# Where the sums of six norms are formed, and in which order the first two weight chunks after a norm are worked through, in a two-block transformer kernel on one Trainium2 core

## The chip, the cores and the metric

The kernel runs on one core of one Trainium2 chip. The metric is the device time of one execution in microseconds (us). The core has TensorE (PE, with its weight loads shown as PEld), VectorE (DVE), ScalarE (ACT), GpSimd (POOL) and the DMA queues, of which SyncE (SP) issues most.

## The reference

Two transformer blocks run one after the other on 512 tokens of 1024 features in float32. The first has sparse and stick-breaking attention, a mixture of 32 experts and a gated per-layer input, and ends with an RMS norm. The second puts 16 meta tokens ahead (528 tokens) and has two layers:

```python
h = jnp.concatenate([meta, x], axis=1)
for l in range(DEPTH_2):
    ...
    h = _layernorm(DN_ALPHA * h + mix, ln_mix_g[l], ln_mix_b[l])
    f = jnp.square(jax.nn.relu(h @ mlp_w1[l])) @ mlp_w2[l]
    h = _layernorm(DN_ALPHA * h + f, ln_mlp_g[l], ln_mlp_b[l])
return h[:, N_META:]

def _layernorm(x, g, b):
    mu = jnp.mean(xf, axis=-1, keepdims=True)
    xc = xf - mu
    var = jnp.mean(jnp.square(xc), axis=-1, keepdims=True)
    return (xc * lax.rsqrt(var + EPS_2) * g + b).astype(x.dtype)

def _rmsnorm(x, g):
    y = xf * lax.rsqrt(jnp.mean(xf * xf, axis=-1, keepdims=True) + EPS)
    return (y * g.astype(jnp.float32)).astype(x.dtype)
```

The change concerns the four layer norms of the second block and two RMS norms of the first: the one ahead of the router (`ffn_norm`) and the final one.

## The kernel before, in words

**Layout.** Features lie on the 128 partitions, so an activation is 8 tiles of 128 features by 512 or 528 tokens: `X` (`residual`), `HN` (`normed`); `XA` and `HA` are their last 512 columns. A sum over the features goes over partitions and over 8 tiles. PE forms it with a matrix of ones (`ONES`) as weights: 8 matmuls of 512 columns, or 16 of 264 (two halves of 528), add up in one PSUM bank or two, and every partition has the sum. A float32 matmul stands as two records in the trace; one on rounded `fp32r` operands as one.

**Weights.** They come in chunks of 128 x 1024 (8 feature tiles by 128 outputs) through a ring `RING` of 8 slots. SP refills a slot when PE has begun the chunk after the one in it (`chunk_begun`).

**High and low parts.** In the last two thirds of the second block (both MLPs and the odd layer's projections) every product is three cheap `fp32r` matmuls: high weight by high activation, low weight by high activation, high weight by low activation. ACT makes a weight chunk's high half (`high`, L1553), POOL subtracts it for the low half (`low_parts`, L2237), PE waits for that in `take_parts` (L420). ACT and POOL convert a chunk while PE works on the one before: `high` waits until chunk n-1 has begun. The places (`IN_MLP`, `IN_ODD`) hold two chunks.

**A layer norm** (PE L760 or L770, ACT L1534, DVE L1620):
1. DVE adds each output tile to the residual (`accumulate`, L1611) as PE finishes it.
2. After the last chunk PE sums the 8 residual tiles (L766 for 512 columns, L780 for 528).
3. DVE scales the sum to the mean in SBUF (L1624, L1626), then subtracts it from each tile (L1628).
4. ACT squares each tile (L1540), PE sums the squares (`norm_sum`, L469), ACT forms the inverse deviation with Ln and Exp (L1188, L1189).
5. ACT converts the first chunk of the next stage (L1557); DVE scales the tiles (L1634); for each tile ACT adds the bias twice, for `X` (L1548) and rounded for `XH` or `XHO` (L1550), and DVE subtracts to get the low half (L1639).
6. PE takes the first chunk of the next stage tile by tile (`fresh`): for each of the 8 it waits for the low half, then does all three products.

The four are called here mix 0, MLP 0 (528 tokens), mix 1 and MLP 1 (512 tokens). MLP 1 ends the kernel, and has only steps 1 to 4, the scaling and one bias.

**The two RMS norms.** ACT squares each residual tile when DVE has added it (L1182, L1295); PE sums the 8 squares after the stage's last chunk, at L574 and L642 through `norm_sum`.

**MLP.** 16 chunks up, 16 down, twice. In the up part ACT evacuates with Relu (L1571, L1573), and DVE squares and splits (L1785 to L1787).

The order on each engine is the order of the code; semaphores alone tie them.

## Time and profile before

| | |
|---|---|
| runs, median of 3 | 2762.01 us (2761.5 to 2762.05) |
| the profiled execution | 2744.34 us, span 2742.6 us |
| PE busy | 2586.7 us, 94% of the span, 11768 matmuls |
| DVE, ACT, POOL busy | 788.4, 693.1 and 597.0 us (29%, 25%, 22%) |
| granted TensorE clock, mean | 0.96 of full speed |
| DMA | 275.33 MB, 100 GB/s on average |

PE is at 94%, but this is a mean over stages. A norm is a place at which PE has, for some 20 us each time, only sums and waits, and there the rows of the timeline tell what is waited for. All rows quoted further down are from the profiled execution.

### The profile page before, as it was taken

The numbers are of one execution on the slowest core, as the hardware profiler recorded it, in microseconds if no ns is written. First come the engines' busy times: TensorE is split into PE (matmuls) and PEld (weight loads), VectorE is DVE, ScalarE is ACT, GpSimd is POOL, SyncE is SP. The second block draws the span as 40 slices with busy tenths as digits, with TensorE's granted clock in tenths as the row PEclk, the third lists the DMA queues.
The fourth block names the chain that finished last, engine by engine and source line by source line (L and its number), as shares of the span: only waits on it lengthen the run. The fifth ranks groups of instructions, "written<-read, shape, count | busy, mean of one in ns | idle before, by whom it ended". The sixth has DMA issues, their size and how long they took to land.

```text
span 2742.6 us, 30358 instructions
## 1 busy us (share of the span) xinstructions
PE 2586.7 (94%) x11768; PEld 1758.7 (64%) x11768; DVE 788.4 (29%) x1294; ACT 693.1 (25%) x1116; POOL 597.0 (22%) x362
## 2 busy tenths in 40 slices
PE   7999999899799979998989999989999999899998
PEld 3446554445433334785679999978877567677875
DVE  0551332111311122234136216135100231640622
ACT  1302224410111121145232222132322231421222
POOL 0000001110011100011004344324433013344442
PEclk9799998899799989999999999999999999999999
DMA  3121110034589952220012222222222012222220
GB/s 139 47 77 65 42 49 10 0 118 174 221 324 356 387 238 70 73 77 8 31 39 93 85 91 86 84 70 93 93 84 77 24 43 81 71 91 92 92 92 31
DMA packets 68261, 275.33 MB, mean 100 GB/s; under 512 B 12440, under 2 KB 12568, under 8 KB 55872
## 3 DMA queue, kind: packets, MB, share of 16 engines
q1 hardware_dynamic: 59648, 260.01, 25.7%
q0 software_dynamic: 8512, 13.89, 1.5%
q8 instruction: 74, 1.21, 0.2%
q14 instruction: 27, 0.22, 0.0%
HBM read 321.02 MB, written 16.80 MB: 123 GB/s over the span
## 4 chain that ended last, share of the span: by engine, by line
PE 45%; issue 22%; POOL 6%; DVE 1%; ACT 1%; DMA 1%; POOLq 0%; SPq 0%; DVEq 0%
PE ps L739 14%; PE ps L754 13%; PE ps L1121 6%; POOL weights_low L2243 5%; PE ps L723 3%; PE ps L1143 3%; PE ps L637 2%; PE ps L469 1%; PE ps L1107 1%; PE ps L661 1%; PE ps L629 1%; DMA area<-pair_rows 0%; POOL parts L2243 0%; PE ps L1129 0%; PE ps L780 0%
## 5 line engine op out<-in xcount | busy, mean ns | idle before, releaser
L754 PE MATMUL ps<-parts 128*128 128x512 f32 x1920 | 486.1, 398 | 26.1 <-DVE parts L1639 13.6
L2243 POOL TENSOR_TENSOR parts<-weights,parts 128x1024 fp32r<-128x1024 f32 x128 | 325.5, 2543 | 632.2 <-ACT parts L1557 632.2
L739 PE MATMUL ps<-parts 128*128 128x264 f32 x3328 | 425.9, 286 | 16.2 <-DVE parts L1787 6.8
L754 PEld LDWEIGHTS ps<-parts 128*128 128x128 f32 x1920 | 364.7, 190 | 118.2 <-issue 24.5
L739 PEld LDWEIGHTS ps<-parts 128*128 128x128 f32 x3328 | 417.7, 191 | 17.7 <-issue 15.6
L1557 ACT ACTIVATE parts<-weights 128x1024 fp32r<-128x1024 f32 x192 | 202.8, 1056 | 427.3 <-PE ps L739 155.5
L2243 POOL TENSOR_TENSOR weights_low<-weights,parts 128x1024 fp32r<-128x1024 f32 x64 | 156.5, 2445 | 317.8 <-ACT parts L1557 317.8
L1121 PE MATMUL ps<-area,normed 128*64 128x512 f32 x752 | 172.8, 601 | 1.6 <-DVE normed L1975 1.6
L1787 DVE TENSOR_TENSOR parts<-normed,parts 128x528 f32 (+1 forms) x64 | 159.0, 2484 | 9.4 <-DVE normed L1786 2.1
L458 PE MATMUL ps<-normed,weights 128*128 128x512 f32 x288 | 125.7, 599 | 3.1 <-DVE normed L1609 2.4
L1121 PEld LDWEIGHTS ps<-area,normed 128*64 128x64 f32 x752 | 56.3, 139 | 112.5 <-issue 110.3
L1022 PE MATMUL ps<-normed,weights 128*128 128x512 f32 x256 | 121.0, 616 | 0.0
L1617 DVE SCALAR_TENSOR_TENSOR residual<-residual,ps 128x528 f32<-128x528 f32 (+3 forms) x32 | 22.3, 696 | 295.0 <-PE ps L739 90.2
L458 PEld LDWEIGHTS ps<-normed,weights 128*128 128x128 f32 x288 | 55.2, 192 | 73.5 <-issue 70.8
L919 PE MATMUL ps<-parts 128*128 128x512 f32 (+1 forms) x320 | 99.8, 393 | 0.8 <-ACT area L1378 0.8
L723 PE MATMUL ps<-residual,weights 128*128 128x264 f32 x416 | 93.4, 386 | 2.6 <-DVE residual L1609 2.4
L1193 ACT ACTIVATE area<-ps 128x512 f32<-128x512 f32 (+2 forms) x71 | 42.1, 599 | 195.0 <-PE ps L458 117.2
L723 PEld LDWEIGHTS ps<-residual,weights 128*128 128x128 f32 x416 | 78.9, 190 | 17.1 <-issue 3.8
L1143 PE MATMUL ps<-area 128*64 128x512 f32 x376 | 87.7, 599 | 1.3 <-DVE area L1983 1.3
L1615 DVE TENSOR_TENSOR residual<-residual,ps 128x512 f32<-128x512 f32 (+2 forms) x32 | 21.5, 691 | 230.1 <-PE ps L739 91.2
L1022 PEld LDWEIGHTS ps<-normed,weights 128*128 128x128 f32 x256 | 47.1, 194 | 62.3 <-issue 61.8
L2120 POOL TENSOR_SCALAR_AFFINE_SELECT area<-area 128x128 f32<-128x128 f32 x68 | 20.2, 304 | 298.2 <-DVE area L1859 243.2
(371 smaller groups left out, 3180.7 us busy)
## 6 DMA issues: line engine op xcount, KB each, us to landing
weights<-in_weights SPq DMA_DIRECT2D x283, 512.0 KB, 3.5
area<-in_experts SPq DMA_DIRECT2D x141, 1024.0 KB
area<-pair_rows SPq DMA_DIRECT2D x4, 1024.0 KB, 8.0
residual<-in_x SPq DMA_DIRECT2D x1, 2048.0 KB, 9.7
area<-bias_scratch POOLq DMA_DIRECT2D x1, 2048.0 KB, 8.6
token_rows<-area SPq DMA_DIRECT2D x1, 2048.0 KB, 6.6
out_tiles<-residual SPq DMA_DIRECT2D x4, 512.0 KB, 2.8
area<-in_decay POOLq DMA_DIRECT2D x2, 528.0 KB, 3.8
```

Source lines behind the costliest of these rows:

```text
L458: ins = mm(ps[:, b], wt[:, k], rhs(k), start=k == 0, stop=k == DT - 1)
L637: ins = mm(ps[:, 4 + n], wt[:, k], HA[:, k], start=k == 0, stop=k == DT - 1)
L723: ins = mm(ps[:, b + h, 0:HALF], wt[:, k], rhs(m * DT + k)[:, HALF * h:HALF * h + HALF], start=m == k == 0, stop=m == len(chunks) - 1 and ...
L739: ins = mm(ps[:, b + h, 0:HALF], wt[:, k], x[:, m * DT + k, HALF * h:HALF * h + HALF], start=m == k == j == 0, stop=m == chunks - 1 and k ...
L754: ins = mm(ps[:, b], wt[:, k], x[:, m * DT + k, META:T2], start=m == k == j == 0, stop=m == chunks - 1 and k == DT - 1 and j == 2)
L919: ins = mm(ps[0:kw, banks[j]], x[:, 2 * m + k, c:c + kw], wt[:, 512 * k:512 * k + 512], start=m == k == n == 0, stop=m == 3 and k == 1 and ...
L1022: ins = mm(ps[:, 5 + (u // 2) % 2], gate.wt[:, k], HA[:, k], start=k == 0, stop=k == DT - 1)
L1121: ins = mm(ps[WIN * side:WIN * side + WIN, n % 2], XW[n % 2][:, 4 * j + k, WIN * side:WIN * side + WIN], wt, start=j == k == 0, stop=j == ...
L1143: ins = mm(ps[WIN * side:WIN * side + WIN, 4 + h], HIDT[n % 2][:, f, WIN * side:WIN * side + WIN], wt, start=f == 0, stop=f == 1)
L1557: fn(place[0][n % 2], RING[:, n % SLOTS], ACT.Copy).then_inc(S["w_hi"], 1)
L1787: v.tensor_tensor(FL[:, at, first:T2], f, FH[:, at, first:T2], ALU.subtract).then_inc(S["dve_evac"], 1)
L2243: g.tensor_tensor(low, RING[:, n % SLOTS], place[0][n % 2], ALU.subtract).then_inc(S["w_lo"], 1)
```

## The change

1. **Feature sums by DVE.** The new `total` lets DVE add up tiles 0 to 6 in `R` while PE is still in the stage; PE sums `R` and tile 7 alone. The matrix is `MEAN` (1/1024 instead of 1), and DVE subtracts straight from PSUM, without the step that scaled the mean.
2. **Two RMS sums in two groups.** The same for the squares: `rms_sum`.
3. **Four chunks converted ahead.** `IN_MLP` holds four high halves, low halves go to `RING_LOW`. Before a layer norm ACT and POOL convert the next stage's first four chunks, without waiting on `chunk_begun`. In the up part ACT evacuates tile j, then converts chunk j + 4.
4. **First two chunks together.** `first_pair`: PE waits for the high half of each activation tile and does both high products for both chunks; then the low activation products of both. ACT makes the eight high halves first, the eight `X` tiles after; DVE scales all eight tiles, then makes the eight low halves from `HN` and the bias in one step each.

The core of the diff:

```diff
@@ the places
-        FH, FL = part(0, 16, N2), part(8448, 16, N2)
-        XH, XL = part(16896, DT, N2), part(21120, DT, N2)
-        IN_MLP = [[part(25344 + D * j, D) for j in range(2)], [part(25344 + D * (2 + j), D) for j in range(2)]]
+        XH, XL = part(0, DT, N2), part(4224, DT, N2)
+        FH, FL = part(12544, 16, N2), part(20992, 16, N2)
+        IN_MLP = [[part(8448 + D * j, D) for j in range(4)], None]
+        EARLY = {use_of("odqk") + 2 + j: part(D * j, D) for j in range(2)}
@@ PE
-                norm_sum(8, SEQ, 7, lambda t: HN[:, t])
+                rms_sum(HA[:, DT - 1])
...
-                norm_sum(8, SEQ, 7, lambda t: MERGED[:, t], at=0)
+                rms_sum(MERGED[:, DT - 1])
...
+            def first_pair(high, low, place, cols):
+                banks = [2 * bank() for _ in range(2)]
+                pair = [take_parts(place) for _ in range(2)]
+                for k in range(DT):
+                    pe.wait_ge(S["x_hi"], w.next("x_hi"))
+                    for c in range(2):
+                        for h, at, width in cols:
+                            for j in range(2):
+                                ins = mm(ps[:, banks[c] + h, 0:width], pair[c][j][:, k], high[:, k, at:at + width],
+                                         start=k == j == 0, stop=False)
...
+                for c, k in [(c, k) for k in range(DT - 2) for c in range(2)] + [(c, k) for c in range(2) for k in (DT - 2, DT - 1)]:
+                    if c == 0:
+                        pe.wait_ge(S["x_lo"], w.next("x_lo"))
+                    for h, at, width in cols:
+                        ins = mm(ps[:, banks[c] + h, 0:width], pair[c][0][:, k], low[:, k, at:at + width],
+                                 start=False, stop=k == DT - 1)
...
+            def layer_norm(cols):
+                pe.wait_ge(S["sum_part"], w.next("sum_part"))
+                for j, src in enumerate((R, X[:, DT - 1])):
+                    if j:
                         pe.wait_ge(S["dve_evac"], w.value("dve_evac"))
-                    ins = mm(ps[:, 0], ONES, XA[:, t], start=t == 0, stop=t == DT - 1)
+                    for h, at, width in cols:
+                        x = R[:, at - cols[0][1]:at - cols[0][1] + width] if j == 0 else src[:, at:at + width]
+                        ins = mm(ps[:, h, 0:width], MEAN, x, start=j == 0, stop=j == 1)
                 ins.then_inc(S["norm_sum"], 1)
...
+            def rms_sum(last):
+                pe.wait_ge(S["sum_part"], w.next("sum_part"))
+                mm(ps[:, 7], ONES, R[:, 0:SEQ], start=True, stop=False)
+                pe.wait_ge(S["norm_sq"], w.next("norm_sq", 8))
+                mm(ps[:, 7], ONES, last, start=False, stop=True).then_inc(S["norm_sum"], 1)
@@ ACT
+                act.wait_ge(S["lru_done"], 4)
+                for j in range(4):
+                    high(use_of("up0") + j, slots=-1)
                 layer_norm("mix", 0)
...
+                act.wait_ge(S["y_lo"], 16)
+                for j in range(4):
+                    high(use_of("up1") + j, slots=-1)
                 layer_norm("mix", 1)
...
-                if kind == "mix":
-                    high(use_of(f"up{l}"))
-                elif l == 0:
-                    high(use_of("odqk"), place=IN_ODD)
+                parts = XH if kind == "mix" else XHO if l == 0 else None
+                if parts is not None:
+                    for t in range(DT):
+                        act.wait_ge(S["norm_out"], w.next("norm_out"))
+                        fn(parts[:, t, T2 - T:], h[:, t], ACT.Identity, bias=vec(f"ln_{kind}_b", 8 * l + t)).then_inc(S["x_hi"], 1)
...
@@ ACT, mlp
-                            high(n + j, i)
                             if w.counted("dve_evac", 7):
...
                             w.count("dve_evac")
+                            high(n + j, i)
...
-                for j in range(7):
+                for j in range(4):
                     high(n - 8 + j)
+                if l == 0:
+                    for j in range(4):
+                        high(use_of("odqk") + j, place=IN_ODD, slots=-1)
                 layer_norm("mlp", l)
@@ DVE
+            def total(n, x, T, name, waits):
+                if 1 <= n < DT - 1:
+                    dve.wait_ge(S[name], waits)
+                    ins = v.tensor_tensor(R[:, 0:T], x[:, 0] if n == 1 else R[:, 0:T], x[:, n], ALU.add)
...
             def layer_norm(kind, l):
-                    step(v.tensor_scalar(two(R[:, :]), halves(0), 1.0 / D, None, ALU.mult))
                 for t in range(DT):
-                    v.tensor_tensor(h[:, t], x[:, t], R[:, 0:T], ALU.subtract).then_inc(S["ln_cent"], 1)
+                        ins = v.tensor_tensor(two(h[:, t]), two(x[:, t]), halves(0), ALU.subtract)
...
-                        v.tensor_tensor(low, x[:, t - 2], high, ALU.subtract).then_inc(S["x_lo"], 1)
+                        v.scalar_tensor_tensor(out=low, in0=h[:, t], scalar=vec(f"ln_{kind}_b", 8 * l + t), in1=high,
+                                               op0=ALU.add, op1=ALU.subtract).then_inc(S["x_lo"], 1)
...
+                v.tensor_scalar(MEAN, NONES, -1.0 / D, None, ALU.mult)
...
                     accumulate(XA[:, n], ps[:, n % 4], 1.0)
+                    total(n, HA, SEQ, "norm_sq", 8 + 1 + n + 1)
...
                     accumulate(XA[:, n], HT[n % 2], 1.0)
+                    total(n - 1, MERGED, SEQ, "norm_sq", 8 + 1 + 8 + 8 + n)
...
                     accumulate(two(X[:, n]), halves(2 * (n % 4)), ALPHA)
+                    total(n, X, T2, "dve_evac", w.next("dve_evac"))
```

The order of the instructions changes at three places that the prediction speaks of.

PE at mix 0, before (`area` is the stage's last operand, `residual` is `X`, `parts` the high and low halves):

```order
L723 MATMUL ps<-area,weights 128x264 x128
L780 MATMUL ps<-residual,matrices 128x264 x16
L469 MATMUL ps<-residual,matrices 128x264 x16
L739 MATMUL ps<-parts 128x264 x768
L135 UNCONDITIONAL_BRANCH
```

and with the change (`rstd` is `R`; the pair of rows at L771 comes 32 times in all):

```order
L729 MATMUL ps<-area,weights 128x264 x128
L796 MATMUL ps<-rstd,matrices 128x264 x2
L796 MATMUL ps<-residual,matrices 128x264 x2
L474 MATMUL ps<-residual,matrices 128x264 x16
L771 MATMUL ps<-parts 128x264
L771 MATMUL ps<-parts,weights_low 128x264
...
L779 MATMUL ps<-parts 128x264 x32
L743 MATMUL ps<-parts 128x264
L743 MATMUL ps<-parts,weights_low 128x264
```

The first sum falls from 16 matmuls to 4. The first two chunks are 64 products with high activations and then 32 with low ones.

DVE at mix 0, before:

```order
L1617 SCALAR_TENSOR_TENSOR residual<-residual,ps 128x528 x8
L1626 TENSOR_SCALAR rstd<-ps 128x528
L1628 TENSOR_TENSOR normed<-residual,rstd 128x528 x8
L1634 SCALAR_TENSOR_TENSOR normed<-normed,vectors,rstd 128x528 x3
L1639 TENSOR_TENSOR parts<-residual,parts 128x528
L1634 SCALAR_TENSOR_TENSOR normed<-normed,vectors,rstd 128x528
L1639 TENSOR_TENSOR parts<-residual,parts 128x528
```

and with the change:

```order
L1654 SCALAR_TENSOR_TENSOR residual<-residual,ps 128x528
L1661 TENSOR_TENSOR rstd<-rstd,residual 128x528
L1654 SCALAR_TENSOR_TENSOR residual<-residual,ps 128x528
L1674 TENSOR_TENSOR normed<-residual,ps 128x528 x8
L1679 SCALAR_TENSOR_TENSOR normed<-normed,vectors,rstd 128x528 x8
L1688 SCALAR_TENSOR_TENSOR parts<-normed,vectors,parts 128x528 x8
```

Six additions stand between the accumulations, the scaled mean is gone, and the low halves come after all scalings.

ACT at MLP 0, before:

```order
L1557 ACTIVATE parts<-weights 128x1024 x7
L1535 ACT_TABLE_LOAD
L1540 ACTIVATE residual<-normed 128x528 x8
L1188 ACTIVATE rstd<-ps,vectors 128x528
L1189 ACTIVATE rstd<-rstd 128x528
L1557 ACTIVATE parts<-weights 128x1024
L1548 ACTIVATE residual<-normed,vectors 128x528
```

and with the change:

```order
L1593 ACTIVATE parts<-weights 128x1024 x8
L1570 ACT_TABLE_LOAD
L1575 ACTIVATE residual<-normed 128x528 x8
L1215 ACTIVATE rstd<-ps,vectors 128x528
L1216 ACTIVATE rstd<-rstd 128x528
L1581 ACTIVATE parts<-normed,vectors 128x528 x8
L1585 ACTIVATE residual<-normed,vectors 128x528 x8
```

The conversion that stood between the inverse deviation and the biases now stands ahead of the norm.

## Rows read from the trace of the kernel before

**Rows 1.** The page, busy time of each engine.
```profile
PE 2586.7 (94%) x11768; PEld 1758.7 (64%) x11768; DVE 788.4 (29%) x1294; ACT 693.1 (25%) x1116; POOL 597.0 (22%) x362
```
**Rows 2.** Timeline, mix 0: start us, length us, engine, line, operation [idle before, releaser].
```profile
1402.93 7.28 PE L780 MATMUL ps<-residual,matrices 128*128 128x264 f32 x32
1403.13 0.70 DVE L1617 SCALAR_TENSOR_TENSOR residual<-residual,ps 128x528 f32<-128x528 f32 x1 [6.42 <-PE ps L723]
...
1410.99 5.04 DVE L1628 TENSOR_TENSOR normed<-residual,rstd 128x528 f32<-128x528 f32 x8
...
1412.43 9.08 PE L469 MATMUL ps<-residual,matrices 128*128 128x264 f32 x32 [2.22 <-ACT residual L1540]
...
1422.28 0.64 ACT L1189 ACTIVATE rstd<-rstd 128x528 f32<-128x528 f32 x1
1422.83 1.04 ACT L1557 ACTIVATE parts<-weights 128x1024 fp32r<-128x1024 f32 x1
1422.95 4.22 DVE L1634 SCALAR_TENSOR_TENSOR normed<-normed,vectors,rstd 128x528 f32<-128x528 f32 x3 [6.92 <-ACT rstd L1189]
...
1427.94 8.93 PE L739 MATMUL ps<-parts 128*128 128x264 f32 x48 [6.43 <-DVE parts L1639]
...
1438.50 11.76 PE L739 MATMUL ps<-parts 128*128 128x264 f32 x95 [1.63 <-POOL parts L2243]
```
**Rows 3.** Timeline, MLP 0.
```profile
1825.00 5.04 DVE L1628 TENSOR_TENSOR normed<-residual,rstd 128x528 f32<-128x528 f32 x8
...
1834.60 0.64 ACT L1189 ACTIVATE rstd<-rstd 128x528 f32<-128x528 f32 x1
...
1850.82 0.50 PE L754 MATMUL ps<-parts 128*128 128x512 f32 x1 [1.67 <-POOL weights_low L2243]
```
**Rows 4.** Timeline, mix 1, and the chain of waits: up chunks 2 to 16.
```profile
2337.07 0.63 ACT L1189 ACTIVATE rstd<-rstd 128x512 f32<-128x512 f32 x1
...
2342.65 8.70 PE L754 MATMUL ps<-parts 128*128 128x512 f32 x24 [6.34 <-DVE parts L1639]
...
2353.04 83.68 PE ps L754 x360
```
**Rows 5.** Timeline, MLP 1, the end of the kernel.
```profile
2715.38 7.03 PE L766 MATMUL ps<-residual,matrices 128*128 128x512 f32 x16
...
2723.17 4.90 DVE L1628 TENSOR_TENSOR normed<-residual,rstd 128x512 f32<-128x512 f32 x8
...
2733.13 5.39 DVE L1634 SCALAR_TENSOR_TENSOR normed<-normed,vectors,rstd 128x512 f32<-128x512 f32 x8 [5.06 <-ACT rstd L1189]
2733.92 5.36 ACT L1548 ACTIVATE residual<-normed,vectors 128x512 f32<-128x512 f32 x8 [0.82 <-DVE normed L1634]
```
**Rows 6.** Timeline, the sums of squares ahead of the router and of the final norm.
```profile
661.46 0.63 ACT L1182 ACTIVATE normed<-residual 128x512 f32<-128x512 f32 x1 [6.24 <-DVE residual L1615]
661.52 7.10 PE L469 MATMUL ps<-normed,matrices 128*128 128x512 f32 x16 [0.83 <-issue]
...
1104.00 7.11 PE L469 MATMUL ps<-area,matrices 128*128 128x512 f32 x16 [2.25 <-issue]
```
**Rows 7.** PE by stretches: us, PE busy (records), granted clock, DMA share, GB/s.
```profile
1412.40:1421.50 9.10, 9.07 (x32) 0.81 0.00 0
...
1427.90:1437.00 9.10, 8.91 (x48) 0.69 0.17 58
...
1826.40:1833.80 7.40, 7.36 (x32) 1.00 0.35 135
...
1529.20:1535.00 5.80, 5.80 (x35) 0.72 0.27 92
```
**Rows 8.** Timeline, one tile of the up part of the first MLP.
```profile
1521.64 2.72 POOL L2243 TENSOR_TENSOR parts<-weights,parts 128x1024 fp32r<-128x1024 f32 x1 [3.07 <-ACT parts L1557]
1522.25 2.67 DVE L1787 TENSOR_TENSOR parts<-normed,parts 128x528 f32 x1
1525.81 0.61 ACT L1573 ACTIVATE normed<-ps 128x528 f32<-128x528 f32 x1 [4.24 <-PE ps L739]
```

159 lines of the change are left out of this document (83 added, 76 removed).

## The prediction

> **What bounds the kernel now.** The page comes first: PE is busy 94% of the span [rows 1], so what is not PE's work gains nothing unless PE waits for it. The waits sorted by releaser and the chain of waits then lead to the norms. There the timeline shows, at mix 0 [rows 2]: when its last chunk is done, PE sums 8 residual tiles for 7.28 us. After that it waits for the centring and the first square, sums the squares, waits 6.43 us for the first low half, and does the first chunk in 8.93 us, although 48 such matmuls take 5.88 us when nothing holds them (95 take 11.76 in the last row: 0.1225 us each is used below, 0.12 to 0.125 with its ends). It then waits another 1.63 us for POOL, which converts the second chunk late. The same pattern is at MLP 0 and mix 1 [rows 3, 4], and its first half at the end of the kernel [rows 5]. Two RMS norms have the long sum alone [rows 6]. All this is on the path: PE is the engine that ends last, and it waits or sums there.
>
> **1. The residual sum and the scaled mean.** Before, from the end of the last chunk (1402.93) to the start of the centring (1410.99) mix 0 needs 8.06 us. With the change PE has the sum of tiles 0 to 6 before the last chunk ends, if DVE's six additions stay hidden: each is a tile operation like those of 0.70 us, in gaps of 6.42 us between accumulations [rows 2]. PE sums `R` in 4 records, 4 x 7.28 / 32 = 0.91 us, beside DVE's last accumulation, which ends at 1403.83. With 0.1 us for the semaphore and 0.91 us for tile 7, the centring starts at 1404.95: 6.0 us sooner. MLP 0 has the same 528 columns: 6.0. With 512 columns [rows 5] it is 2723.17 - 2715.38 = 7.79 us before, and 0.2 + 0.70 + 0.1 + 2 x 7.03 / 16 = 1.9 us after: 5.9 each at mix 1 and MLP 1. **Sum 23.8 us.** The centring from PSUM takes 0.70 us a tile (the accumulation that reads PSUM) instead of 0.63 [rows 2]. PE's sum of squares takes 0.91 us a tile and stays the slower one, so this costs the first tile's 0.07 us, counted as nothing.
>
> **2. The first two chunks.** Count from the end of Exp, s.
> - Before: mix 0 has s = 1422.92, and its second chunk ends at 1438.50 + 5.88 = 1444.38, s + 21.5. MLP 0: s = 1835.24; the second chunk starts at 1850.82, and 24 matmuls of 0.232 us (83.68 / 360, [rows 4]) end at 1856.4, s + 21.2. Mix 1: s = 2337.70, end 2353.04 + 5.6 = 2358.6, s + 20.9.
> - After: the first scaling is done at s + 0.8 and ACT's first high half at s + 1.55 (the last norm's two rows start 0.03 and 0.82 after its Exp, at 0.67 a tile [rows 5]). PE starts at s + 1.65. Then 96 matmuls follow without a gap: 11.8 us for 528 columns, and 48 of 0.232, 11.1 us, for 512. The ends are s + 13.4 and s + 12.8.
> - Why no gap: in the high phase PE needs 8 x 0.1225 = 0.98 us a tile and gets one every 0.7. The low halves begin at s + 5.6 (8 scalings) and are all there at s + 11.3. PE comes to tile 7 of the first chunk at about s + 12. The four conversions are done ahead, so no POOL operation of 2.72 us [rows 8] stretches the scalings, as one does now, where three take 4.22 us instead of 2.1 [rows 2].
>
> Gains 8.1, 8.4 and 8.1: **24.6 us.** Chunk 5 is due at s + 25; its conversion starts after the first evacuation (s + 14) and needs 1.04 + 2.72 us. It is late by nothing. The late `X` biases (eight of ACT's, until about s + 12.5) end before that evacuation.
>
> **3. The two RMS sums.** 16 records take 7.10 us [rows 6]. After: the router's `R` sum runs 661.52 to 662.4, while the last square ends at 662.09; the end is 663.3 instead of 668.6, gain 5.3. At the final norm the sixth addition stands on DVE behind the last accumulation, with which PE's start at 1104.00 is tied, and adds 0.7 before PE may start; two matmuls then end at 1106.5 instead of 1111.1, gain 4.6. **9.9 us.** The router and the experts follow in sequence, with PE's own waits, so I let this pass through whole.
>
> **4. The clock.** PE's idle time costs more than itself. The granted clock is 0.81 during the square sum of mix 0, which takes 9.08 us for 7.3 of work, and 0.69 in the first chunk after; after the 3.4 us stop between up and down part it is 0.72 for 5.8 us, 1.6 us lost [rows 7]. These are mixtures of 2.4 and 1.2 GHz. Now low clock in the first chunk is covered, as PE waits for low halves anyway. With the change PE starts sooner, is dense, and pays: bounds are 0 (at MLP 0 the square sum, behind a 2.2 us wait too, ran at 1.00 [rows 7]) and 3.4 us, twice the 1.6. I take 1.3 at each of three pairs, nearest the 1.6 row, 1.2 at the even layer's start, where 7.1 us of PE work ahead becomes 1.8, 0.2 at the router and 0.8 over the four square sums. **Cost 6.1 us.**
> The Trainium skill (TensorE: Matmul & The Clock Gate, "HAM oscillation — how this bites in real kernels") says that waits between bursts of matmuls throttle the engine again at each burst. It speaks against this change, which shortens the bursts between unchanged waits, and is the first rival.
>
> **5. At nothing:** the 12 early conversions (ACT and POOL work that moves, hidden behind stages of eight or more chunks); the swap of evacuation and conversion in the up part, since the trace shows that order in effect already, `chunk_begun` holding the conversion back; POOL's three DMA issues at MLP 0, behind four more conversions at most. `total` at mix 1 is the exception: five conversions run back to back there, 5 x 2.72 us, over the last two chunks. DVE's two-SBUF operation beside POOL takes 2.67 instead of 0.7 us [rows 8], so the sixth addition can be late by up to 3 us: kept for the range. The centring reads one operand from PSUM, as the accumulations do that show 0.70 us.
>
> **Sum:** 23.8 + 24.6 + 9.9 - 6.1 = 52.2 us. The profiled execution, 2744.3 us, becomes 2692. The median of the runs lies 17.7 us above it, 0.6%; I take the same distance, so 2762.0 - 52.2 = **2709.8 us**.
>
> **Rivals.**
> - *The clock takes the gain back (15%).* Every square sum and every pair runs at 1.2 GHz: 4 x 3.5 us (half of 7.3 us' work done at half speed), 3 x 3.4, and 1.7 each at router and even layer, 28 us instead of my 6. Time 2762 - 58 + 28 = 2732. For it: mix 0 shows 0.81 even after a long sum. Against: behind the same wait it was 1.00 at MLP 0 [rows 7], and at MLP 1 the 9.96 us from the first centring to the scalings leave room for a sum at full speed alone [rows 5].
> - *The clock costs nothing (10%).* The 58.3 us come whole, and mix 0's square sum gets its 1.7 us back: 2702.
> - *Conversion and split collide for good: slower (3%).* In the up part DVE's split of a tile ends with POOL's conversion, at 1524.92, and the next evacuation is done at 1526.4 [rows 8]; 1.5 us is free. If the new order or the ring's shorter lead of four chunks pushes ACT, POOL or DVE over PE's 5.8 us a chunk by x, each of 64 up chunks pays x. It outweighs 52 us from x = 0.8. At x = 1.0 the time is 2762 + 12 = 2774. Against: POOL needs 2.7 of the 5.8 us.
> - *The gain is absorbed (2%).* Were the sums' time covered by another wait, as a router or expert stage that waits for DMA, parts 1 to 3 would give little: 2760.
> - *The forecast (70%)*, 2702 to 2722.
>
> The Trainium skill (SBUF — State Buffer, "SBUF: two separate sides") says that a GpSimd operation and a VectorE one with two SBUF inputs exclude each other for a whole instruction; rows 8 agree. By it alone mix 1 would be 2 to 3 us later, 2712.
>
> **How the numbers follow.** Point 2710. The bounds of the clock term (0 to 28) and mix 1's 3 us give 2702 to 2735; leaving out the tail of the first rival and all below 2700, the range is 2700 to 2726, for 80%. A change within 0.2% (5.5 us) is about what this kernel's measurement can't tell from none. Faster by more: forecast, both clock rivals and half a percent of others, 0.95; same 0.02; slower 0.03.
>
> **What would show it.** In the new profile: 4 records (528) or 2 (512) of `MEAN` ahead of each centring, started within 2 us after the last chunk; no scaled mean; first-pair matmuls from 1.7 us after Exp and both chunks done 13 us after it; no wait on POOL there; 4 records instead of 16 at the RMS sums; the granted clock of the square sums and pairs says what part 4 costs. Wrong would be: a PE wait for `R`; waits on high halves between tiles; a new wait on POOL in the up part; or a clock at 0.5 through a whole pair.

## The result

| | before | after |
|---|---|---|
| runs, median | 2762.03 us (2761.5 to 2767.18, 4 runs) | 2693.43 us (2691.6 to 2693.95, 4 runs) |
| the profiled execution | 2744.34 us, span 2742.6 us | 2693.95 us, span 2692.2 us |
| granted TensorE clock, mean | 0.96 | 0.96 |

The change makes the kernel faster, ratio 0.9746 (95% interval 0.9729 to 0.9763), by 68.6 us. 2710 us was forecast, 2700 to 2726 as the range: the time lies 6.6 us below it. Yet between the two profiled executions there are only 50.4 us, against a forecast sum of 52.2. The rest of this text is about these two figures.

The page of the changed kernel, first part (before: [rows 1]):

```profile
PE 2555.0 (95%) x11672; PEld 1740.8 (65%) x11672; DVE 811.0 (30%) x1327; ACT 692.9 (26%) x1116; POOL 596.5 (22%) x362
```

PE has 96 records less and is busy for 31.7 us less; the rest of the 50.4 us was waiting. Timeline of the changed kernel at mix 0 (before: [rows 2]; start us, length us, engine, line, operation [idle before, releaser]):

```profile
1401.90 1.05 PE L796 MATMUL ps<-rstd,matrices 128*128 128x264 f32 x4
1402.11 0.70 DVE L1654 SCALAR_TENSOR_TENSOR residual<-residual,ps 128x528 f32<-128x528 f32 x1 [5.61 <-PE ps L729]
1402.86 1.16 PE L796 MATMUL ps<-residual,matrices 128*128 128x264 f32 x4
1404.06 5.01 DVE L1674 TENSOR_TENSOR normed<-residual,ps 128x528 f32<-128x528 f32 x8 [1.25 <-PE ps L796]
...
1405.49 7.39 PE L474 MATMUL ps<-residual,matrices 128*128 128x264 f32 x32 [1.47 <-ACT residual L1575]
...
1413.65 0.64 ACT L1216 ACTIVATE rstd<-rstd 128x528 f32<-128x528 f32 x1
1414.33 5.52 DVE L1679 SCALAR_TENSOR_TENSOR normed<-normed,vectors,rstd 128x528 f32<-128x528 f32 x8 [5.26 <-ACT rstd L1216]
1415.13 5.49 ACT L1581 ACTIVATE parts<-normed,vectors 128x528 fp32r<-128x528 f32 x8 [0.84 <-DVE normed L1679]
1416.01 0.56 PE L771 MATMUL ps<-parts 128*128 128x264 f32 x1 [3.13 <-ACT parts L1581]
```

From the start of PE's sum to the centring it is 2.16 us in place of 8.06. The three scalings that took 4.22 us beside POOL are now part of eight that take 5.52, and PE opens the pair 1.7 us after the end of Exp. The squares keep the shape they had. The centring from PSUM takes 5.01 us for eight tiles, 0.63 each as before, where 0.70 had been taken.

Mix 1, at the point where `total` was thought to come late (before: [rows 4]):

```profile
2286.52 2.87 DVE L1661 TENSOR_TENSOR rstd<-rstd,residual 128x512 f32<-128x512 f32 x1
...
2290.97 1.02 PE L796 MATMUL ps<-rstd,matrices 128*128 128x512 f32 x2
2291.17 0.69 DVE L1654 SCALAR_TENSOR_TENSOR residual<-residual,ps 128x512 f32<-128x512 f32 x1 [1.78 <-PE ps L991]
```

The sixth addition is stretched to 2.87 us beside POOL, as [rows 8] had led one to fear, but PE is still in the last chunk, and the stretch costs nothing.

The two RMS sums of the changed kernel (before: [rows 6]; the rows of L1215 are ACT's Ln, which waits for the sum; the router's is L1188 at 668.66 in the kernel before):

```profile
667.75 0.63 ACT L1209 ACTIVATE normed<-residual 128x512 f32<-128x512 f32 x1 [6.17 <-DVE residual L1652]
669.81 0.69 ACT L1215 ACTIVATE rstd<-ps,vectors 128x512 f32<-128x512 f32 x1 [1.43 <-PE ps L808]
...
1104.53 1.33 PE L806 MATMUL ps<-rstd,matrices 128*128 128x512 f32 x2 [2.93 <-DVE rstd L1661]
1105.65 1.91 PE L808 MATMUL ps<-area,matrices 128*128 128x512 f32 x2
1107.61 0.69 ACT L1215 ACTIVATE rstd<-ps,vectors 128x512 f32<-128x512 f32 x1 [2.91 <-PE ps L808]
```

PE by stretches in the changed kernel, with the granted clock behind POOL's column (before: [rows 7]; columns: us, then the busy time of PE, PEld, DVE, ACT and POOL with their counts, granted clock, DMA share, GB/s). They are mix 0's squares, the opening of its pair, and the openings of the pairs of MLP 0 and mix 1:

```profile
1405.40:1412.90 7.50, 7.39 (x32) 6.00 (x32) 3.67 (x6) 4.34 (x8) 0.00 (x0) 1.00 0.01 2
1416.00:1419.30 3.30, 3.29 (x15) 3.30 (x16) 3.30 (x6) 3.30 (x6) 0.00 (x0) 0.50 0.40 148
...
1814.70:1818.00 3.30, 3.23 (x9) 2.54 (x10) 3.30 (x6) 3.30 (x6) 0.00 (x0) 0.58 0.43 145
...
2304.70:2308.00 3.30, 3.30 (x14) 2.69 (x15) 3.30 (x6) 3.30 (x6) 0.00 (x0) 1.00 0.46 154
```

Two pairs open at about half clock, one does not, and the square sum of mix 0, at 0.81 before, is at 1.00. One place that the prediction priced at 1.2 us stands out: the even layer's projections, right behind the final norm. Their first 10 us in the kernel before, in the changed kernel, and in a second trace of the changed kernel (a0 below), each from its own first matmul:

```profile
1113.49:1123.49 10.00, 10.00 (x45) 8.57 (x46) 9.66 (x18) 0.61 (x1) 5.15 (x6) 1.00 0.49 149
1109.95:1119.95 10.00, 9.99 (x33) 8.11 (x34) 9.66 (x18) 0.00 (x0) 5.15 (x6) 0.72 0.41 134
1108.65:1118.65 10.00, 10.00 (x32) 8.13 (x33) 9.66 (x18) 0.00 (x0) 5.15 (x6) 0.72 0.40 134
```

### The profile page after: what moved, and what is told of

Its sections match the earlier page's. It is cut to its first block, busy times and chain, and to the rows that moved or that the text cites. A ratio compares the mean times of both kernels' runs of the same rounds, so it can differ in the third digit from the quotient of the medians.

```text
span 2692.2 us, 30120 instructions
## 1 busy us (share of the span) xinstructions
PE 2555.0 (95%) x11672; PEld 1740.8 (65%) x11672; DVE 811.0 (30%) x1327; ACT 692.9 (26%) x1116; POOL 596.5 (22%) x362
## 3 DMA queue, kind: packets, MB, share of 16 engines
q1 hardware_dynamic: 59648, 260.01, 26.1%
## 4 chain that ended last, share of the span: by engine, by line
PE 66%; issue 3%; DVE 2%; POOL 2%; ACT 1%; DMA 1%; SPq 0%; DVEq 0%; POOLq 0%; ACTq 0%
PE ps L756 15%; PE ps L743 13%; PE ps L1148 6%; PE ps L729 6%; PE ps L946 4%; PE ps L991 3%; PE ps L1170 3%; PE ps L642 2%; PE ps L973 2%; POOL weights_low L2301 2%; PE ps L474 1%; PE ps L893 1%; PE ps L909 1%; PE ps L771 1%; PE ps L962 1%
## 5 line engine op out<-in xcount | busy, mean ns | idle before, releaser
L2301 POOL TENSOR_TENSOR weights_low<-weights,parts 128x1024 fp32r<-128x1024 f32 x192 | 481.8, 2512 | 898.3 <-ACT parts L1593 898.3
L756 PE MATMUL ps<-parts 128*128 128x512 f32 x1344 | 422.3, 394 | 9.0 <-DVE parts L1842 6.7
L743 PE MATMUL ps<-parts 128*128 128x264 f32 x2240 | 409.9, 285 | 8.1 <-DVE parts L1842 6.9
L743 PEld LDWEIGHTS ps<-parts 128*128 128x128 f32 x2240 | 348.4, 189 | 8.7 <-issue 8.7
L743 PE MATMUL ps<-parts,weights_low 128*128 128x264 f32 x1120 | 318.6, 284 | 0.0
L756 PEld LDWEIGHTS ps<-parts 128*128 128x128 f32 x1344 | 253.3, 188 | 70.1 <-issue 10.4
L756 PE MATMUL ps<-parts,weights_low 128*128 128x512 f32 x672 | 266.2, 396 | 0.0
L743 PEld LDWEIGHTS ps<-parts,weights_low 128*128 128x128 f32 x1120 | 212.5, 190 | 0.0
L756 PEld LDWEIGHTS ps<-parts,weights_low 128*128 128x128 f32 x672 | 126.4, 188 | 29.4
L1654 DVE SCALAR_TENSOR_TENSOR residual<-residual,ps 128x528 f32<-128x528 f32 (+1 forms) x32 | 22.3, 696 | 282.2 <-PE ps L743 90.1
L463 PEld LDWEIGHTS ps<-normed,weights 128*128 128x128 f32 x288 | 54.6, 190 | 72.6 <-issue 70.1
```

What stands on the lines that cost most here:

```text
L463: ins = mm(ps[:, b], wt[:, k], rhs(k), start=k == 0, stop=k == DT - 1)
L743: ins = mm(ps[:, b + h, 0:HALF], wt[:, k], x[:, m * DT + k, HALF * h:HALF * h + HALF], start=m == k == j == 0, stop=m == chunks - 1 and k ...
L756: ins = mm(ps[:, b], wt[:, k], x[:, m * DT + k, META:T2], start=m == k == j == 0, stop=m == chunks - 1 and k == DT - 1 and j == 2)
L2301: g.tensor_tensor(RING_LOW[:, n % SLOTS], RING[:, n % SLOTS], high_slot(n, place), ALU.subtract).then_inc(S["w_lo"], 1)
```

## The experiments

**Both kernels again.** The distance between the profiled execution and the median, which the forecast had carried over, was tried first.

> The kernel before, unchanged, to learn why its timed executions lie at 2762 us and its profiled one at 2744 us, a distance I had carried over to the changed kernel, which does not have it. Theory 1 (execution by execution the TensorE clock falls at other places, above all in the attention stages from 243 to 547 us, where PE waits a little in each unit): the executions spread between 2744 and 2767 us, and the slower ones have a mean granted clock 0.01 lower; the profile's stages differ in length where the granted clock differs. Theory 2 (something outside the clock that only this kernel has, in one stage): all executions near 2762 us at the clock 0.96, and one stage is about 18 us longer than in the earlier profile at the same granted clock. Theory 3 (the first profile was shortened by chance of the launch, not by a stage): stages of equal length, span and time apart by more than 2 us.

Measured: 2755.22 us (2749.77 to 2769.45, 12 runs) against 2753.41 (2744.42 to 2766.84, 17 runs) of the same kernel: ratio 1.001 (0.999 to 1.0031). The kernel before has no one time. Over the comparisons of this study it was timed 103 times more: 12 executions lie at 2744.0 to 2745.6 us with mean granted clock 0.960, 44 at 2749.6 to 2756.0 with 0.956 or 0.957, 11 at 2757.0 to 2759.4 with 0.954 or 0.955, and 36 at 2761.5 to 2773.1 with 0.947 to 0.951. The profiled one of the forecast was of the first kind, the runs beside it of the last. The five comparisons ran on five chips, and in each the executions of one kernel spread over at least 19 us, so that the spread is not one between chips. This is theory 1.

The trace taken here is of the second kind (2751.79 us). At the router's sum it is 3.4 us behind the first profile, at the first score 4.7, and 7.5 when the scores and what follows them at once are done; that is its whole distance. The last step, before and here (the matmuls right behind the scores):

```profile
1267.85 2.77 PE L827 MATMUL ps<-matrices,area 128*97 128x128 f32 x24 [0.95 <-DVE area L2086]
1273.60 4.51 PE L827 MATMUL ps<-matrices,area 128*97 128x128 f32 x24 [0.95 <-DVE area L2086]
```

> The changed kernel, unchanged, for more executions. The kernel before gave 2744 to 2769 us in 29 executions, its time falling with the mean granted clock (0.960 at 2744, 0.948 at 2769). Theory 1 (chance of the draws: both kernels have the same attention stages, in which the clock varies): the changed kernel spreads likewise, from about 2690 to 2712, median near 2700, and the gain is about 52 us as worked out from the two profiles. Theory 2 (the change also ends the spread): all executions lie within 3 us of 2693, and the gain is 60 us against the median of before.

Measured: 2693.22 us (2687.37 to 2695.99, 6 runs), before 2761.93 (17 runs), ratio 0.9757 (0.9723 to 0.9792). The changed kernel's ten executions lie within 9 us, those of the kernel before within 29. That is nearer to theory 2 (all within 3 us of 2693) than to theory 1 (2690 to 2712). So the gain is 57 us from fastest to fastest, 50 from profile to profile, and near 69 between these medians.

**The parts alone.** Sums only (feature sums and RMS sums, the rest as before); early conversion and the pair only; early conversion only.

```diff
@@ a1, from the kernel before
-                norm_sum(8, SEQ, 7, lambda t: HN[:, t])
+                rms_sum(HA[:, DT - 1])
...
-                layer_norm()
+                layer_norm(HALVES)
@@ a2, from the changed kernel
-                rms_sum(HA[:, DT - 1])
+                norm_sum(8, SEQ, 7, lambda t: HN[:, t])
...
+                for t in range(DT):
...
+                        ins = mm(ps[:, h, 0:width], ONES, X[:, t, at:at + width], start=t == 0, stop=t == DT - 1)
@@ a3, from a2
-                first_pair(XHO, XLO, IN_ODD, TOKENS)
-                for n in range(6):
-                    linear_parts(1, XHO, XLO, IN_ODD)
+                for n in range(8):
+                    linear_parts(1, XHO, XLO, IN_ODD, fresh=n == 0)
```

> Parts 1 and 2 alone (feature sums and squares added up by VectorE, mean in the matrix); chunks, conversion and first chunk as before. My working: 23.8 us from the four layer norms and 8 to 10 from the two RMS sums, so 30 to 33 us less than before, and in the profile the centring starts about 2.1 us after the last chunk's end instead of 8.06. Rival (the gain of the sums is mostly given back, since less TensorE work ahead lets the clock fall in the square sums and first chunks): 20 us or less, with granted clocks of 0.5 to 0.8 in the four square sums.

> Parts 3 and 4 alone (four chunks ahead, high products of two chunks first), sums as before. My working: second chunk done 13 to 15 us after Exp instead of 21, at three norms: 20 to 25 us less than before. If the parts add up, this and the sums alone give 52 together. Rival (the two parts interact: with a long sum ahead the clock holds through the pair): 25 us here, and more than the whole change has left over.

> Part 3 alone: four chunks converted ahead, but the first chunk tile by tile as before, with all three products, ScalarE and VectorE in the old order, old sums. Removed are the first conversion behind Exp (1 us of ScalarE, 2.7 us of GpSimd that held up three scalings by 2.1 us) and the wait for the second chunk (1.6 us): 3 x (2.1 + 1 + 1.6), some 12 to 14 us less than before, if the clock doesn't change. Rival (the second chunk's wait was covered by something else that now shows, the first chunk at 1.3 us a tile): 8 us or less.

Measured: a1 2719.28 us (2713.66 to 2720.2, 6 runs), ratio 0.9849 (0.9815 to 0.9884); a2 2735.51 (2723.75 to 2745.26, 6), 0.9905 (0.9868 to 0.9942); a3 2743.57 (2740.28 to 2756.88, 12), 0.9954 (0.9928 to 0.9979). The fastest execution of each, against 2744.4 for the fastest kind of the kernel before, has clean parts: 30.7, 20.6 and 4.1 us. The first two are as expected, and agree with what the traces show of the places themselves (below). a3 is a miss: 12 to 14 us were expected and its rival had 8 or less. Its trace has the second chunk of mix 0 done 18.5 us after Exp (1463.0) in place of 21.5, 3.0 us gained where 4.7 were worked out: the wait for the second chunk is gone, but the first still takes until 12.7 us after Exp, 1.2 us less than before. Three such norms would give 9 us; where the other 5 went is not shown. The pair makes 16 us more out of the early conversion.

The traces of the two slowest, a2 and a3, share a stretch that no other trace had until then. Groups of PE instructions between 1210 and 1330 us, the score matmuls of the even layer's attention (`pe_mla`, 40 tasks): before, then a2, then the changed kernel (busy us, mean ns | idle before, releasers):

```profile
L816 PE MATMUL ps<-area 96*16 96x16 f32 (+5 forms) x96 | 25.1, 382 | 6.9 <-DVE area L2086 5.5 <-ACT area L1305 0.8
```

```profile
L834 PE MATMUL ps<-area 96*16 96x16 f32 (+5 forms) x96 | 40.6, 588 | 6.4 <-DVE area L2127 5.6 <-ACT area L1323 0.8
```

```profile
L843 PE MATMUL ps<-area 96*16 96x16 f32 (+5 forms) x96 | 24.9, 381 | 6.9 <-DVE area L2143 5.5 <-ACT area L1332 0.8
```

The same 96 records take 15.5 us more. PE by stretches, 1240 to 1270 us, before and in a2:

```profile
1240.00:1270.00 30.00, 23.83 (x101) 13.76 (x101) 20.94 (x82) 16.05 (x25) 6.41 (x7) 1.00 0.00 1
```

```profile
1240.00:1270.00 30.00, 26.10 (x62) 14.59 (x61) 13.52 (x55) 13.74 (x22) 7.65 (x8) 0.50 0.00 1
```

The clock is 1.00 (2.4 GHz) in the one and 0.50 (1.2 GHz) in the other. Nothing of the change acts here. PE sits idle 0.8 us ahead of the scores, for ACT's last evacuation, and up to 0.8 us in each of the eight heads, for DVE.

**Does the RMS part, or the start of the scores, decide it?** The RMS part alone, the layer norm part alone (both as in the diffs above), and matmuls ahead of the scores that put them off:

```diff
@@ c3 (n = 5), c4 (n = 10, kernel before), d1 (n = 2)
                 pe.wait_ge(S["k_ready"], 1)
+                for _ in range(n):
+                    mm(ps[:, 4, 0:HALF], IDENT, X[:, 0, 0:HALF], start=True, stop=True)
                 for u in range(5 * HEADS):
```

> The kernel before with the two RMS sums in two groups alone. Seven traces so far show what parts the executions of a kernel: in the two at the lowest mean clock (2743.5 and 2754.0 us of span) the forty score tasks of the even stage's attention ran at granted clock 0.50 from 2.5 us after their first matmul on, and the score matmuls took 46.2 us; in the five others they took 31.1 to 32.3 us. Theory A (the start of the scores decides): the RMS sums move the start of the scores by some us, and no execution falls into the slow kind: 2744.4 (the fast kind of the kernel before) less 8.5 = 2736 median, all of its executions within 2731 to 2745, though the median of the kernel before lies 5 to 18 us above its fast kind. Theory B (the parts only add up, the spread is chance): as many slow ones as before, 8.5 us under the median of the kernel before, executions spread over 20 us or more.

> The changed kernel with the two RMS sums as they were; the scores of the even stage's attention start then where they do in the kernel before. Theory A (the start of the scores decides): both kinds occur, 2744.4 less 46 = 2698 where the scores keep their clock and some 15 us more, 2713 to 2718, where they lose it; spread of the executions over 12 us, median more than 8.5 us above the changed kernel's. Theory B (the parts only add up): 2693.4 and 8.5 = 2702 us, within 5 us like the changed kernel.

> The changed kernel with five matmuls of 128x264 more, into a bank that nobody reads, right ahead of the first score matmul of the even stage's attention: 1.2 us of work (0.24 us each, from the 32 such matmuls that take 7.66 us ahead of them). Theory A (the start of the scores decides): they push the start of the scores to where the two slow traces had it; the scores take 46 us in place of 31, and the time is 2693.4 and 1.2 and 15 = 2710 us in all or most executions. Theory B: 2694.6 us, scores 31 us. If neither, the clock does not depend on the start to a microsecond.

> The kernel before with ten such matmuls more at the same place: 2.4 us of work. Theory A (the start of the scores decides): the scores of most executions start past the bad spot (which spans a microsecond or two) and the time falls in spite of the work: median 2747 to 2752, under that of the kernel before, scores 31 us in the trace. Theory B: slower by 2.4 us, the same spread as the kernel before. A third outcome, all slow (2764 and more), would say that the bad spot is wider than 2.4 us.

Measured: c1 2747.28 us (2737.72 to 2752.3, 12 runs); c2 2711.67 (2702.13 to 2719.34, 6); c3 2691.45 (2687.38 to 2702.4, 6); c4 2756.54 (2751.43 to 2771.64, 12), beside 2752.16 for the kernel before. c2 came as theory A had it, with three executions at 2702 to 2706 us and three at 2717 to 2719. The others did not. c1 should by theory A have been free of the stretch, and its trace has it in full (96 records, 40.7 us; 2750.94 us); its fastest executions, 2737.7, are 6.7 us under the fastest of the kernel before. c3 did not lose the clock: its trace, of its slowest execution, has the scores at 24.9 us. c4 was slower, by 4.4 us where its ten matmuls take 4.7. Its trace, of a fast execution, has the scores at full clock, but four others lie at 2768 to 2772 with a mean clock of 0.949 or 0.950, 16 to 20 us above its fastest, about what the stretch costs; none of them was traced. So the RMS sums do not cure it, the start alone does not bring it on in the changed kernel, and in the kernel before 4.7 us of dense matmuls between the wait and the scores do not keep it away in every execution. c3 also taught that five such matmuls are 2.49 us, not 1.2: each is two records.

> The changed kernel with two matmuls of 128x264 more ahead of the first score matmul. The trace of the run with five showed that such a matmul is two instructions and takes 0.49 us, so that five were 2.5 us and not 1.2; two are 1.0 us. Theory A (the start of the scores decides, in a spot about a microsecond wide that the five stepped over): the scores take 46 us in place of 31 and the time is 2693.4 and 1 and 15 = 2709 us in most executions. Theory B (the start has nothing to do with it): 2694.4 us, scores 31 us.

Measured: 2694.39 us (2690.63 to 2704.12, 6 runs), scores 24.9 us. Theory A in its first form falls. But the added matmuls, which stand behind the wait of 0.79 us, had also kept PE busy until the scores began. So the idle time itself was put to the test.

**The idle time filled.** One matmul goes into PE's wait ahead of the scores, one into the wait of each head:

```diff
+                pe.wait_ge(S["act_evac"], w.value("act_evac", 1))
+                mm(ps[:, 6, 0:HALF], IDENT, X[:, 0, 0:HALF], start=True, stop=True)
                 pe.wait_ge(S["act_evac"], w.value("act_evac"))
...
+                    if t == 1:
+                        mm(ps[:, 4, 0:HALF], IDENT, X[:, 0, 0:HALF], start=True, stop=True)
                     if u >= 2:
                         pe.wait_ge(S["smax"], w.next("smax"))
```

> The kernel of c1_rms_only, whose scores lost their clock in ten executions of twelve by its times (2743 to 2752 against 2737.7), with one matmul of 128x264 in the 0.79 us in which TensorE waits for ScalarE ahead of the scores, and one in each head ahead of its second score matmul, where TensorE waits 0.8 us for VectorE: nine matmuls of 0.49 us, all but the first head's in idle time. Theory A (TensorE loses its clock there because it does too little as the scores begin): the clock holds, scores 31 to 32 us, median 2738 to 2739 and the executions within 5 us or so of it, 8 or 9 us under c1_rms_only. Theory B (the fall has another cause than the engine's idle time): 2748 us and the same spread as c1_rms_only, and with it TensorE's fillers at half clock on the path, some us more.

> The kernel before with the same nine matmuls. Theory A: its executions at mean clock 0.951 and below (2761 to 2773 us) vanish, the rest stay at 2744 to 2754; median 2745 to 2752. Theory B: 2753 to 2762, spread as before. Should theory A hold here and in d2, the 17.7 us by which the median of the kernel before lay above its profiled execution were this one stretch.

Measured, d3: 2750.29 us, ratio 0.9976 (0.9956 to 0.9996). One execution at 13381 us stands apart and is left out; the other eleven lie at 2744.3 to 2752.0. In the same comparison 10 of 23 executions of the kernel before were at 2757 us and above; at 2761 us and above, where the expectation drew the line, there were five, and by these alone eleven executions would tell little. The traces of d2 and d3 have the scores at full clock (24.8 us). d2: 2743.25 us (2737.67 to 2748.72, 12 runs), 4 us under c1 where 8 or 9 were expected; no execution is in c1's upper range of 2750 to 2752, but seven lie between 2743 and 2749, four of them further off than the 5 us that were allowed. The one profiled there, 2744.19 us, is slow elsewhere (0.956 on the mean). The fillers are a cure for the one stretch and not for the spread as a whole. Which of the nine does it, the first or those in the heads, these two runs do not part.

**The idle time made longer, in the kernel that never lost its clock.** ACT does one (e1) or two (e2) more sigmoids ahead of the evacuation that PE waits for; e3 is e2 with four matmuls in the wait.

```diff
@@ e1 (k = 1), e2 and e3 (k = 2), ACT
-                    evac2([(ALL, out[:, n % 4])], ACT.Sigmoid, bias=vec(bias, n % 4))
+                    evac2([(ALL, JUNK[j]) for j in range(k) if n == 7] + [(ALL, out[:, n % 4])], ACT.Sigmoid, bias=vec(bias, n % 4))
@@ e3, PE
+                pe.wait_ge(S["act_evac"], w.value("act_evac", 1))
+                for _ in range(4):
+                    mm(ps[:, 6, 0:HALF], IDENT, X[:, 0, 0:HALF], start=True, stop=True)
                 pe.wait_ge(S["act_evac"], w.value("act_evac"))
```

> The changed kernel with one more sigmoid of a 128x528 tile on ScalarE (0.70 us by its neighbours in the trace) ahead of the evacuation that the first score matmul waits for; TensorE then sits idle some 1.5 us there in place of 0.79. In the runs with two and five matmuls more at that place the scores began 1 and 2.1 us later and never lost their clock, so the start alone does not decide; but those matmuls also kept TensorE busy up to the scores. Theory A (idle time ahead of the scores and what follows decides): the scores run at half clock, 46 us, in most executions: 2693.4 and 0.7 and 15 = 2709. Theory B (the state that the execution brings from earlier stages decides, and 0.7 us of idle time does not matter): 2694, scores 31 us.

> The same with two such sigmoids: 2.2 us idle. Theory A: 2693.4 and 1.4 and 15 = 2710, in every execution. Theory B: 2695, scores 31 us.

> The kernel of e2 with four matmuls of 128x264 (0.49 us each, 2.0 in all) in those 2.2 us. Theory A: the clock holds, scores 31 us, 2695 us in every execution, some 15 us under e2, by work that does nothing but keep TensorE busy. Theory B: the same as e2, whichever that is.

Measured: e1 2694.83 us (2685.06 to 2696.88, 5 runs), e2 2718.66 (2714.93 to 2719.5, 5 runs), e3 2695.94 (2692.11 to 2710.75, 6 runs). Timeline of PE at the first scores in e1:

```profile
1235.20 0.66 PE L843 MATMUL ps<-area 96*16 96x16 f32 x4 [1.38 <-ACT area L1332]
1236.03 2.81 PE L843 MATMUL ps<-area 96*128 96x272 f32 x10 [0.17 <-DVE area L2143]
1239.63 3.13 PE L843 MATMUL ps<-area 96*128 96x144 f32 x12 [0.80 <-DVE area L2143]
```

in e2:

```profile
1234.79 0.66 PE L843 MATMUL ps<-area 96*16 96x16 f32 x4 [1.97 <-ACT area L1332]
1235.62 3.69 PE L843 MATMUL ps<-area 96*128 96x272 f32 x10 [0.17 <-DVE area L2143]
1240.09 5.04 PE L843 MATMUL ps<-area 96*128 96x144 f32 x10 [0.78 <-DVE area L2143]
```

and in e3:

```profile
1232.73 2.05 PE L834 MATMUL ps<-residual,matrices 128*128 128x264 f32 x8
1234.80 0.66 PE L846 MATMUL ps<-area 96*16 96x16 f32 x4
1235.62 2.80 PE L846 MATMUL ps<-area 96*128 96x272 f32 x10 [0.17 <-DVE area L2146]
```

e2 and e3 start the scores at the same time, 1234.8, a hair from the changed kernel's own. With 1.97 us of idle time ahead of them the clock goes, 2.5 us after the first score, and all five executions are slow (2715 to 2720 us; one was traced); filled, it stays, and five of six are at 2692 to 2698 (the sixth, 2710.75, may have lost it; its trace was not taken). ACT's two sigmoids are in both, so their own work is not what costs. With 1.38 us, in e1, no execution lost it, where theory A expected most to. The price of the stretch in e2 against e3 is 22.7 us: 15.7 in the score matmuls, the rest in the 30 us after them, where the clock of e2 is still at 0.50 in part.

```profile
L843 PE MATMUL ps<-area 96*16 96x16 f32 (+5 forms) x96 | 40.6, 587 | 7.6 <-DVE area L2143 5.6 <-ACT area L1332 2.0
```

**The clock at the norms.** The changed kernel with small matmuls in PE's waits in the four layer norms:

```diff
                 ins.then_inc(S["norm_sum"], 1)
+                warm(WARM[0])
...
                     norm_sum(8, SEQ, 7, lambda t: X[:, t])
+                warm(WARM[1])
...
+            WARM = (4, 9)
...
+            def warm(n):
+                for _ in range(n):
+                    mm(ps[:, 4, 0:P], MEAN, MEAN, start=True, stop=True)
```

> The changed kernel with small matmuls (128x128, some 0.3 us each, into a bank that nobody reads) while TensorE waits in each of the four layer norms: four between the sums and the squares (1.5 us idle) and nine behind the squares (3.1 us idle). In the traces of the changed kernel the 15 matmuls that open the pair of mix 0 ran at granted clock 0.50 (0.42 us apiece spaced 0.22) and those of MLP 0 at 0.58, mix 1 at 1.00. Theory A (the idle time ahead of them costs the clock): both are back at 1.00, 1.6 us each, some 3 us in all: 2690. Theory B (the fall is settled before the norm, or the fillers delay the squares): no gain, 2693 to 2696.

Measured: 2693.43 us (2687.64 to 2698.9, 6 runs), the same as without. PE by stretches in this kernel, the pairs of mix 0 and MLP 0:

```profile
1416.00:1419.30 3.30, 3.30 (x30) 3.30 (x29) 3.30 (x6) 3.30 (x6) 0.00 (x0) 1.00 0.50 159
1814.70:1818.10 3.40, 3.40 (x17) 2.75 (x16) 3.40 (x7) 3.40 (x7) 0.00 (x0) 1.00 0.47 154
```

Theory A's clock came true at both pairs, 1.00 in place of 0.50 and 0.58, and the time did not move. The 1.6 us of mix 0 are gone again at MLP 0's norm (398.5 us from sum to sum, 398.8 without the fillers); those of MLP 0 are kept until mix 1 (488.7 us for 490.3) and lost in the last MLP (381.4 for 379.7). The next wait, 3.4 us between up and down part, is where most of the first is lost. The 7 us behind it, each from its own first matmul, in d4, in the changed kernel and in e1, which has no fillers:

```profile
1511.67:1518.67 7.00, 7.00 (x36) 7.00 (x37) 0.00 (x0) 1.06 (x1) 2.36 (x1) 0.59 0.23 75
1514.08:1521.08 7.00, 7.00 (x45) 7.00 (x46) 0.00 (x0) 1.06 (x1) 2.36 (x1) 0.76 0.21 75
1515.63:1522.63 7.00, 7.00 (x36) 7.00 (x37) 0.00 (x0) 1.06 (x1) 2.37 (x1) 0.59 0.22 75
```

d4 has 0.59 where the changed kernel has 0.76. But e1, c3 and d1 have 0.59 there too, with their pairs of mix 0 at 0.50. That the fillers at the pairs brought on the fall behind the next wait is therefore not shown; it comes without them as well. No version tried here beats the changed kernel by more than the runs can tell; c3's 2691.45 us overlaps it.

## Why the prediction was wrong

**What held.** The sum of 52.2 us met 50.4 between the profiled executions, in part by luck, as will be seen; its steps can be read one by one.

- *Part 1, 23.8 us.* Sum start to centring went from 8.06 to 2.16 us at mix 0 and MLP 0, and from 7.79 to 2.10 at MLP 1 (2670.69 to 2672.79); mix 1 shows the same 2.10. That is 23.2.
- *Part 2, 24.6 us, less 3.9 for the clock at the pairs.* From the end of Exp to the end of the second chunk: 15.0 us at mix 0 (the third chunk begins at 1429.28), 14.5 at MLP 0, 12.9 at mix 1, against 21.5, 21.2 and 20.9. That is 21.2 where the net forecast was 20.7. Mix 1, at full clock, meets the 12.8 of the forecast. No wait on POOL is left there.
- *Part 3, 9.9 us.* Router 5.15, from 7.14 us between PE's start and Ln (661.52 to 668.66) to 1.99 (667.82 to 669.81); final norm 3.4 where 4.6 was expected, since its second matmul ran at half clock (1.91 us for 0.9) and PE waited 2.93 us for the sixth addition, 0.7 more than before. A wait of PE for `R` was on the prediction's list of signs that it is wrong; here it cost what the sum had for it.
- *Part 4, 6.1 us lost.* Measured are 4.3, put together otherwise. At the pairs it was 3.3 us: 1.6 and 1.7 at the first two, nothing at the third. The square sums cost nothing and gave 1.7 us back at mix 0. The even layer's start cost 2.7 us where 1.2 was taken: from Ln of the final norm to the first score it is 127.2 us (1107.61 to 1234.83; 127.3 in a0) in place of 124.5 (1111.14 to 1235.63), with a granted clock of 0.72 in place of 1.00 in its first 10 us. That the shorter sum ahead brings this on, as the prediction had it, is not shown: c1 has the same short sum and takes 124.5 us. Both clock rivals, 28 us and none, were off.
- *Part 5.* Nothing late at mix 1, and no new wait in the up part.

The places add up to 51.9 us, beside 52.2 in the forecast. Profile to profile it is 50.4, since the two executions also differ where the kernels do not: the router's sum, the first changed place, began at 661.5 us in the kernel before and 667.8 in the changed one, with a granted clock of 0.82 and 0.76 in the attention stage from 430 to 560 us. Of these 6.3 us 4.8 came back in later stages that the change leaves alone. That they nearly cancel is luck.

**What failed** is the step "The median of the runs lies 17.7 us above it, 0.6%; I take the same distance". That distance was no constant of the measurement, and neither a rival nor the range allowed for its being another in the changed kernel. The forecast's profiled execution was of the fastest kind of a kernel that has at least four. The changed kernel's median is its profiled time, 2693.4 against 2693.95, and the forecast from the profiled time alone, 2692, would have been right to 1.5 us.

**What the 17.7 us were.** For the most part, as these runs suggest, the half clock in the scores of the even layer. Shown: the stretch is in the traces of three kernels that share the code there with the kernel before, and costs 15.5 us in the score matmuls; with matmuls in the idle time the upper executions of the kernel before are not seen (d3, 0 of 11 at 2757 us and above, against 10 of 23); and in the changed kernel more idle time brings the stretch on in all of five executions and filling it takes it off in five of six at least (e2, e3). Inferred: no execution of the kernel before above 2752 us was itself profiled, so that its 2762 us are this stretch follows from d3, not from a trace. The 7.5 us between its first kind and the trace at 2751.79 are not this stretch: they lie in the attention stages, at the even layer's start and in the matmuls behind the scores.

**What stays open** is why, at the same 0.79 us of idle time, c1, a2 and a3 lose the clock, and by their times some executions of the kernel before and of c2 too, and the changed kernel in none of ten. Its two traces have the scores begin at 1233.6 and 1234.8 us, and of two starts within half a microsecond of the latter e2's lost the clock and e1's did not; d1's, at 1234.0 with two matmuls between the wait and the scores, did not either, so it is neither the start nor the idle time by itself. The executions of one kernel also differ in where the clock falls in the attention stages; whether that carries through to the scores is not shown. The gain of 69 us is thus 50 to 57 us that the change earned and some 12 to 18 that depend on how this kernel and the chip's clock fall together; against the median of all 103 executions of the kernel before, 2755.35 us, it is 62.

The Trainium skill (TensorE: Matmul & The Clock Gate, "A second HAM failure mode: psum-queue depth-cycling") tells of an engine that idles shortly but often between groups of matmuls and loses its clock by that, not by one long wait. The 0.8 us of idle time in every four of these scores are such a pattern. Here the clock does not go back and forth, though: once down, it stays down through the scores, and by e2 and e3 one wait ahead of them decides whether it goes down, while by the times of c4 dense matmuls right ahead are no sure cure. The Trainium skill's other case (TensorE: Matmul & The Clock Gate, "HAM oscillation — how this bites in real kernels"), the first rival, did not decide here: of three pairs behind a wait of 3.1 us, two opened at 0.50 and 0.58 and one at 1.00.

## What to carry to other kernels

Before a change is priced against a median, look at the single times: where they stand in groups with a mean clock for each, the profiled execution belongs to one group, and the sum worked out from it gives the time of that group and no other. A small gap in TensorE's work ahead of a stage of thin matmuls (96 rows here) with waits between them can cost many times its length (e2), and work that nobody needs, put into the gap, can take the loss away (e3). Full clock at one place does not yet mean less time, so the whole time must be measured, not the place (d4). Stretches of two kernels are compared from the same instruction on, not from the same microsecond.

## What the runs showed of the hardware

- The mean granted clock of an execution tells its time to 5 us: 2744.0 to 2745.6 us at 0.960, 2749.6 to 2752.2 at 0.957, 2751.1 to 2756.0 at 0.956, 2757 to 2759.4 at 0.954 and 0.955, 2761.5 to 2763.4 at 0.950 and 0.951, 2766 to 2770 at 0.948 and 0.949, 2773 at 0.947, over 103 executions of one kernel on one core each of five chips.
- A clock that falls as the scores begin stays at 0.50 through nearly all of them, though PE is busy 87% of the time then (26.1 of 30 us, a2) and 79% when the clock holds (23.8 of 30, before). The scores' busy time grows from 25 to 40.6 us, by a factor of 1.6 and not 2.
- Idle time of 1.97 us ahead of the scores lost the clock in five executions of five (e2), 1.38 us in none of five (e1), 1.97 us filled with matmuls in at most one of six (e3), all in the same kernel.
- Matmuls in PE's waits in the norms gave full clock at both pairs that had lacked it, and the same time of the whole (d4). Behind the next wait of 3.4 us the clock was 0.59 with them and 0.76 or 0.59 without (a0; c3, d1, e1).
- A float32 matmul of 128x264 is two records and takes 0.49 us at full clock (ten records in 2.49 us, c3).
